# A two-layer retention/attention/MoE step: modulation by chunks in the first stage, a split scatter, and norms on two columns

## The chip, the core and the metric

The kernel runs on one core of a Trainium2 chip. A core has five engines with a queue each: PE (TensorE, the matrix engine; its weight loads are listed apart as PEld), DVE (VectorE), ACT (ScalarE), POOL (GpSimd) and SP (SyncE, which here only issues DMAs). They meet through semaphores. All memory traffic runs over 16 DMA engines that the queues share. The metric is the time of one execution on the device in microseconds (us), the median of the runs.

## What is computed

256 tokens (128 of a prompt, 128 of a sample) with 1024 channels go through two layers, everything in float32. Cut to what matters here:

```python
def trunk_layer(x, cond, lw, lam_init, ropes, ctx):
    mod = (jax.nn.silu(cond) @ lw['w_ada'] + lw['b_ada'])[:, None, :]
    shift1, scale1, gate1, shift2, scale2, gate2 = jnp.split(mod, 6, axis=-1)
    h = rmsnorm(x, lw['norm_mix']) * (1 + scale1) + shift1
    mix, new_ctx = token_mixers(h, lw, lam_init, ropes, ctx)   # retention | differential | latent attention
    x = x + gate1 * (mix @ lw['w_out'])
    h = rmsnorm(x, lw['norm_ffn']) * (1 + scale2) + shift2
    x = x + gate2 * moe_ffn(h, lw)                             # 64 experts, 6 per token, and a shared one
    return x, new_ctx
# at the end: y = rmsnorm(x, norm_final), for prompt and sample
```

`w_ada` is 1024 x 6144 in each layer, 24 MB; `w_in` is 1024 x 2208; an expert has three weights of 1 MB, and all 64 experts of both layers are read.

## The kernel before

The order of every engine's work is written out by hand: each engine has one function, and named semaphores tie them together.

**Tiles.** Activations lie transposed: `xT` and `hT` hold eight chunks of 128 channels, each 128 partitions x 256 tokens (prompt and sample beside each other). Weights of the mixer pass through a ring `gu` of four slots of 2 MB. `stream_items` lists the pieces in the order of loading: `("ada", l, q)`, one twelfth of `w_ada` of a layer; `("w_in", l, k)`, 512 columns of `w_in` (k = 2: queries and keys of the differential attention; 3: its values and the query latent; 4: 160 columns, the key latent; 0 and 1: retention); `("mla", l, 0)`, the two up-projections of latent attention; `w_out`; the shared expert. Item n goes into slot n % 4, and SP issues its load only when PE has counted (`weights_used`) the use of item n - 4. SP issues in order, so one waiting load holds back all behind it.

**First stage, layer 0.** DMAs: `xT`, then all constants `cst` (968 KB), then items. Items 0 to 3 are the four quarters of the first third of `w_ada`, by rows: a quarter has 256 of the 1024 input channels for all 2048 columns (shift 1 and scale 1). Only when all four are in PSUM is a modulation value complete. PE does `norm(0)` (the sums of squares by 8 matmuls with a matrix of ones), `ada(0..3)` and a select (L1483: matmuls that sum the four partial rows and turn them), DVE adds the bias and makes `amp`, and ACT (prompt half) and DVE (sample half) modulate the eight chunks of `hT` (L759, L1019). Then `w_in` 2 (queries and keys, 32 matmuls of 256 columns, L1528), `ada` 4 and 5, `w_in` 3 for the prompt (8 matmuls of 512 columns), the differential scores of unit 0 (L1566) with two rotations, `w_in` 3 for the sample (8 more), scores of unit 1 with the turning of the softmax of unit 0 (L1465) between their halves, `ada` 6 and 7, `w_in` 4, and so on.

**The softmax beside it.** Between the scores of unit 0 and those of unit 1 stand a chain on DVE (maximum, rope: `d_roped`) and one over ACT and DVE (`exps(0)`, then `combined(0)`: `p_scaled`). The scores of unit 1 wait for `d_roped`, the turning of unit 0 for `p_scaled`.

**Norms.** `norm(k)`: k = 0 and 2 at the start of a layer, k = 1 and 3 ahead of its experts. For odd k the squares are summed on DVE to one chunk, one matmul with ones spreads the sums over all partitions (L1509), ACT takes the root of 128x256 (L749), DVE the reciprocal (L1011), and the chunks are scaled (L1015) and modulated. PE fills the time with four matmuls of 512 columns (L1518).

**Experts.** Per layer 22 rounds: two with fixed experts, then ten turns of a "quad" (four experts, 32 token slots each) and a "pair" (two experts, 64 slots each). `expert_round` does gate and up (L1954), a gather for the next round (L1886), the scatter of the round before (L1893, 8 matmuls), turns, and down (L1983). SP loads the experts in an order that the routing gave, each part when its buffer is free.

**End.** After the last scatter DVE adds into `xT` (L1440, 16 instructions), PE turns `xT` back (first all chunks of the prompt, then the sample), ACT squares four halves (L964), takes the root (L967), DVE scales with the final gain into a strided layout (L1453, twice 128x1024), and ACT issues two stores (L971).

Of the kernel before, what the change touches and what calls it, by code (L numbers as in the profile page):

```python
# [29 lines left out]
P = 128  # L30
# [44 lines left out]
CONSTS = ["ident", "ones", "rot_d", "rot_m", "cos_d", "sin_d", "cos_m", "sin_m", "fwd", "bwd", "before", "iota", "cols",  # L75
          "order"]
CO = {n: P * i for i, n in enumerate(CONSTS)}
COL = {"i+1": 0, "C-i": 1, "C-1-i": 2, "i": 3, "eps": 4, "sel": 5, "first": 13, "cap": 16}


FIRST_W = len(CONSTS) * P + G * NC_ + DEPTH * 6 * NC_ + 4 * NC_
# [3 lines left out]
def shape_constants():  # L85

    a = np.zeros((P, len(CONSTS), P), np.float32)
    i = np.arange(P)
    a[:, 0] = np.eye(P)
    a[:, 1] = 1.0  # L90
# [19 lines left out]
    a[:, 2], a[:, 4], a[:, 5] = tables(P // DIF_D, 0, DIF_D)  # L110
    a[:, 3], a[:, 6], a[:, 7] = tables(1, MLA_N, MLA_R)
    a[:, 8] = np.maximum(i[None, :] - i[:, None], 0)
    a[:, 9] = np.maximum(i[:, None] - i[None, :], 0)
    a[:, 10] = i[:, None] < i[None, :]
    a[:, 11] = i[None, :] + 1
    a[:, 12, 0], a[:, 12, 1], a[:, 12, 2], a[:, 12, 3], a[:, 12, 4] = i + 1, P - i, P - 1 - i, i, EPS
    for j in range(4):
        for g in range(G):
            a[32 * j + g, 12, 5 + G * j + g] = 1.0

    first = np.maximum(FIXED - i, 0) * 1e6 + (P - i)
    a[:, 12, 13] = first
    cap = np.full(E, PAIR_CAP)
    rank = np.arange(E)
    for m in range(TURNS):
# [3 lines left out]
    a[:, 12, 16:16 + E] = cap  # L129
    a[:, 13, 0:E], a[:, 13, E:2 * E] = first[:E], rank  # L130
    return a.reshape(P, len(CONSTS) * P)
# [5 lines left out]
ADA_AT = [{"P2": [4, 5], "P3": [6, 7], "P4": [8], "UQ": [9], "M": [10, 11], "P0a": [12], "P0b": [13],  # L137
           "P1a": [14], "P1b": [15]},
# [3 lines left out]
THIRD = 2048  # L142


def stream_items():
# [5 lines left out]
    for l in range(DEPTH):  # L151
        if l == 0:
            out += [("ada", n // 12, n % 12) for n in range(4)]
        if 2 * l in ADA_NORM:
            out.append(("ada", 1, ADA_NORM[2 * l] % 12))
        for k in (2, 3, 4):
            out.append(("w_in", l, k))
            ada(l, f"P{k}")
# [14 lines left out]
def trunk(nc, t, out):  # L173
    ctx = ExitStack()
    with ctx:
# [15 lines left out]
        at = CO["order"] + P  # L191
# [107 lines left out]

        key_row, above, chosen = (hit[0:E, E * n:E * n + E] for n in range(3))  # L300
# [47 lines left out]
        def bc(ap, axis, n):  # L348
# [13 lines left out]
            ada_r ada_sel ada_mod  # L362
            sq_ready sq_summed ss_ready std_ready xn_ready h_a h_d amp_ready
# [11 lines left out]
            turned_y y_sq y_ms y_std y_done act_own dve_own""".split()  # L375
# [14 lines left out]
        for l in range(DEPTH):  # L390
            off = 0 if l == 0 else expert_slot[l - 1][1]
            for n in range(starts[l], ends[l]):
                item_slot[n] = (off + n - starts[l]) % RING
# [1721 lines left out]
```

## Time and profile before

| | |
|---|---|
| median of 3 runs | 1363.7 us (1361.63 to 1365.36) |
| the profiled execution's own time | 1363.03 us |
| its span | 1361.0 us |
| PE busy | 1238.2 us (91%) |
| DVE, ACT busy | 283.1 us (21%), 233.1 us (17%) |
| DMA | 496.14 MB, mean 365 GB/s |

The span runs from the first to the last recorded instruction; 2.0 us of the execution lie outside it. The chain of waits goes back from the last instruction to the first, and only what stands in it can shorten the run. In 40 slices of the span the DMA engines read 411 to 422 GB/s while the experts run, and less in the two mixers (154 to 287 GB/s in the slices from 0.08 to 0.17 of the span, 152 to 257 in those from 0.50 to 0.62); the first mixer runs to about 197 us.

### The profile page before, as it was taken

Reading aid. Unit: us, or ns where it says so; the run is one execution under the profiler, and the core shown is the slowest. Engines: PE = TensorE matmul, PEld = TensorE weight load, DVE = VectorE, ACT = ScalarE, POOL = GpSimd, SP = SyncE. Lnnn points to the kernel's source line nnn. Section 1 sums busy time; section 2 is a strip of 40 time slices with the busy share of each in tenths; the row PEclk is TensorE's granted clock in tenths of the full one; section 3 lists DMA queues with packets and bytes.
Section 4 is the critical chain, followed back from the end, with each engine's and each line's share of the span. In section 5 each row is a group of like instructions: output and inputs, shape, how many; then the busy total and the mean of one; then the engine's idle time right before and its main releaser. Section 6 shows DMA issues by size and latency. Waiting matters only on the chain.

```text
span 1361.0 us, 22696 instructions
## 1 busy us (share of the span) xinstructions
PE 1238.2 (91%) x9592; PEld 843.2 (62%) x9592; DVE 283.1 (21%) x714; ACT 233.1 (17%) x516; POOL 2.7 (0%) x13
## 2 busy tenths in 40 slices
PE   4999999999998898889899999999999889888986
PEld 2656578667765565556565658766767565555654
DVE  1253344111010110011033624511011010101012
ACT  1243312110100010000034521311010001000101
POOL 0000000000000000000000000000000000000000
PEclk9999999999998898889999999999999899999988
DMA  9886739899999999999965653999999999999991
GB/s 389 359 346 255 287 154 411 360 421 421 420 421 421 422 421 422 422 422 421 409 231 221 257 213 152 417 372 414 421 420 421 422 421 422 422 422 421 422 414 72
DMA packets 81024, 496.14 MB, mean 365 GB/s; under 512 B 10560, under 2 KB 12864, under 8 KB 24640
## 3 DMA queue, kind: packets, MB, share of 16 engines
q1 hardware_dynamic: 76752, 492.68, 88.3%
q10 hardware_dynamic: 4208, 2.52, 0.6%
q8 instruction: 51, 0.84, 0.2%
q14 instruction: 13, 0.11, 0.0%
HBM read 493.17 MB, written 2.00 MB: 364 GB/s over the span
## 4 chain that ended last, share of the span: by engine, by line
PE 66%; DMA 29%; SPq 2%; DVE 1%; issue 1%; ACT 0%; DVEq 0%
DMA dn<-in_exp_w_down 18%; PE PS L1954 14%; PE PS L1983 12%; PE PS L1528 8%; PE PS L1886 7%; PE PS L1893 6%; DMA gu<-in_exp_w_gate 6%; PE PS L1790 4%; DMA gu<-in_w_in 2%; PE PS L1496 2%; PE PS L1465 2%; PE PS L1852 2%; DMA gu<-in_w_ada 2%; PE PS L1930 1%; SPq L504 1%
## 5 line engine op out<-in xcount | busy, mean ns | idle before, releaser
L1954 PE MATMUL PS<-gu,arena 128*32 128x256 f32 (+1 forms) x3072 | 314.6, 381 | 1.8 <-issue 1.8
L1983 PE MATMUL PS<-arena 128*64 128x512 f32 (+1 forms) x336 | 177.9, 679 | 62.2 <-DMA dn<-in_exp_w_down 60.7
L1954 PEld LDWEIGHTS PS<-gu,arena 128*32 128x32 f32 (+1 forms) x3072 | 185.4, 117 | 78.3 <-issue 19.9
L1983 PE MATMUL PS<-dn,arena 128*32 128x512 f32 (+1 forms) x688 | 185.7, 637 | 0.0
L1886 PE MATMUL PS<-arena 128*128 128x128 f32 x1408 | 176.3, 278 | 0.5 <-ACT arena L936 0.5
L1886 PEld LDWEIGHTS PS<-arena 128*128 128x128 f32 x1408 | 164.1, 192 | 17.9 <-issue 16.7
L1893 PE MATMUL PS<-arena 128*128 128x256 f32 x704 | 159.6, 380 | 1.4 <-ACT arena L918 1.4
L1954 PE MATMUL PS<-arena 128*64 128x256 f32 (+1 forms) x672 | 151.9, 379 | 0.0
L1893 PEld LDWEIGHTS PS<-arena 128*128 128x128 f32 x704 | 130.4, 190 | 19.8 <-ACT arena L918 3.2
L1383 DVE TENSOR_TENSOR arena<-arena,PS 128x256 f32<-128x256 f32 x44 | 18.5, 421 | 558.3 <-ACT arena L932 558.3
L918 ACT ACTIVATE arena<-PS 128x512 f32<-128x512 f32 x88 | 52.6, 597 | 463.5 <-PE PS L1983 463.5
L1983 PEld LDWEIGHTS PS<-arena 128*64 128x64 f32 (+1 forms) x336 | 44.2, 143 | 116.5 <-issue 113.7
L1954 PE MATMUL PS<-xh,arena 128*64 128x256 f32 x352 | 82.1, 387 | 19.3 <-DMA gu<-in_exp_w_gate 19.2
L1954 PEld LDWEIGHTS PS<-arena 128*64 128x64 f32 (+1 forms) x672 | 83.4, 124 | 20.3
L1954 PEld LDWEIGHTS PS<-xh,arena 128*64 128x64 f32 x352 | 47.3, 139 | 55.8 <-DMA gu<-in_exp_w_gate 22.9
L1983 PEld LDWEIGHTS PS<-dn,arena 128*32 128x32 f32 (+1 forms) x688 | 48.3, 127 | 45.6 <-issue 42.8
L1377 DVE COPY arena<-PS 128x512 f32<-128x512 f32 x44 | 30.4, 691 | 214.5 <-PE PS L1465 214.5
L932 ACT ACTIVATE arena<-PS 128x256 f32<-128x256 f32 x44 | 16.9, 384 | 314.3 <-PE PS L1954 314.3
L1528 PE MATMUL PS<-gu,xh 128*128 128x512 f32 (+1 forms) x192 | 66.0, 498 | 0.5 <-DMA gu<-in_w_in 0.5
L1528 PE MATMUL PS<-xh,gu 128*128 128x256 f32 x256 | 60.2, 397 | 3.1 <-DMA gu<-in_w_in 1.9
L1528 PEld LDWEIGHTS PS<-xh,gu 128*128 128x128 f32 x256 | 50.5, 199 | 13.1 <-DMA gu<-in_w_in 4.1
L1496 PE MATMUL PS<-gu,condw 128*32 128x512 f32 x384 | 46.9, 614 | 6.7 <-DMA gu<-in_w_ada 6.1
(241 smaller groups left out, 964.8 us busy)
## 6 DMA issues: line engine op xcount, KB each, us to landing
gu<-in_exp_w_gate SPq DMA_DIRECT2D x106, 1024.0 KB, 16.0
gu<-in_exp_w_up SPq DMA_DIRECT2D x86, 1024.0 KB, 17.6
dn<-in_exp_w_down SPq DMA_DIRECT2D x86, 1024.0 KB, 18.5
gu<-in_w_ada SPq DMA_DIRECT2D x24, 2048.0 KB, 10.7
arena<-in_exp_w_up SPq DMA_DIRECT2D x42, 1024.0 KB, 14.5
arena<-in_exp_w_down SPq DMA_DIRECT2D x42, 1024.0 KB, 16.1
xh<-in_exp_w_gate SPq DMA_DIRECT2D x22, 1024.0 KB, 11.3
gu<-in_w_in SPq DMA_DIRECT2D x8, 2048.0 KB, 12.0
```

The lines of the kernel that those rows point to most:

```text
L918: return A(yy[:, :, half], PS[:, 7 - n, :].rearrange("p (t c) -> p c t", c=NC_), ACT.Copy)
L1377: return v.tensor_copy(turned_back, PS[:, 6, :])
L1383: tt(hh, sact, PS[:, 5, FF:2 * FF], ALU.mult).then_inc(S["hid_ready"], 1)
L1465: return pe.transpose(dst, src, ident[0:parts, 0:parts])
L1496: ins = mmul(PS[32 * j:32 * j + 32, 7, :], condw[:, 2 * quarter + c, :], wv[:, c, 512 * j:512 * j + 512], start=(quarter == 0 and c == 0), ...
L1528: ins = mmul(PS[0:lhs(k).shape[-1], bank, o:o + rhs(k).shape[-1]], lhs(k), rhs(k), start=(k == 0), stop=(k == NC_ - 1))
L1790: ins = mmul(PS[:, wo_bank(c), (c % 2) * T:(c % 2) * T + T], wo[k // 4][:, k % 4, c], mixT[:, k] if k < 4 else latent_T[:, k - 4], start=( ...
L1852: ins = mmul(PS[:, bank, j * T:j * T + T], w[:, u, k, j], hT[:, k, :], start=(k == 0), stop=(k == NC_ - 1))
L1886: ins = mmul(PS[:, 4, (c % 4) * P:(c % 4) * P + P], h_tok[:, g, c], onehot[b][:, g], start=(g == 0), stop=(g == 1))
L1893: ins = mmul(PS[:, c // 2, (c % 2) * T:(c % 2) * T + T], yy[:, c], selT, start=(first and c % 2 == 0), stop=False, skip_group_check=True)
L1954: ins = mmul(PS[w * h:w * h + w, 5, FF * half:FF * half + FF], xg[:, k, w * h:w * h + w], weights[half][:, k], start=(k == 0), stop=(k == ...
L1983: ins = mmul(PS[w * h:w * h + w, 7 - n, :], hidT[:, j * P + w * h:j * P + w * h + w], weights[:, j, 512 * n:512 * n + 512], start=(j == 0) ...
```

## The change

It has four parts.

1. **First stage of layer 0.** The first third of `w_ada` is laid out by columns (`w_ada_first`): a piece has all 1024 input channels for two chunks of 128 channels of shift and scale. PE makes two chunks' modulation from one piece (`chunks(i)`, L1717) and selects it with four matmuls of 2 columns (`chunks_select(i)`, L1725); DVE and ACT then modulate these two chunks. `w_in` 2 and 3 are loaded behind the first two pieces, and PE takes both projections chunk by chunk as `hT` comes (L1738, L1749). The second value product, which stood behind the scores of unit 0, now stands ahead of them. The constants are split: 264 KB first, the other 704 KB (`tables_in`) with the late ones. The `ada` pieces have new places: before, 4 and 5 stood behind `w_in` 2, 6 and 7 behind the scores of unit 1, 8 behind `w_in` 4 and 9 ahead of the last queries; now 4 and 5 behind the scores of unit 1, 6 and 7 behind `w_in` 4, 8 and 9 ahead of the last queries, 12 moves behind the second half of `w_in` 0 and 14 to the end.
2. **Norms 1 and 3.** The sums come as two columns (128x2), root and reciprocal are taken of these, and two matmuls spread them into PSUM; DVE reads the factors there. The four filling matmuls become five, in three places.
3. **Last turn of a layer's experts.** The scatter is split: five of its 8 matmuls between gate and up of the last pair, three behind up. SP issues the last pair's gate and up of its second expert ahead of the down weights of its first.
4. **End.** PE turns `xT` back in the order of the additions. The root's table is loaded ahead of the squares. For the prompt DVE multiplies PSUM by the gain before the root is known, and ACT scales; for the sample one DVE instruction as before. Both read PSUM with a stride of 128 elements and write SBUF in order. ACT and SP store one half each.

```diff
-ADA_AT = [{"P2": [4, 5], "P3": [6, 7], "P4": [8], "UQ": [9], "M": [10, 11], "P0a": [12], "P0b": [13],
-           "P1a": [14], "P1b": [15]},
+ADA_AT = [{"P3": [4, 5], "P4": [6, 7], "UQ": [8, 9], "M": [10, 11], "P0b": [12, 13], "P1b": [14, 15]},
...
+FIRST_USED = [("chunks", 0, 0), ("chunks", 0, 1), ("chunks", 0, 2), ("chunks", 0, 3), ("w_in", 0, 2), ("w_in", 0, 3)]
...
+            out += [("chunks", 0, 0), ("chunks", 0, 1), ("w_in", 0, 2), ("w_in", 0, 3), ("chunks", 0, 2), ("chunks", 0, 3)]
+            ada(l, "P3")
...
                     if n - starts[l] >= RING:
-                        sp.wait_ge(S["weights_used"], n - RING + 1)
+                        sp.wait_ge(S["weights_used"], freed_by[it])
...
+                    queries_and_keys((0, 1, 2, 3))
+                    values_and_latent((0, 1))
+                    chunks(2)
+                    values_and_latent((2,))
+                    chunks_select(2)
+                    values_and_latent((3,))
+                    chunks(3)
+                    queries_and_keys((4, 5))
+                    chunks_select(3)
+                    values_and_latent((4, 5))
+                    queries_and_keys((6, 7), told=True)
+                    values_and_latent((6, 7), told=True)
...
+                for g in range(G):
+                    ins = mmul(PS[:, 5, 2 * g:2 * g + 2], hT[:, 0, g * P:g * P + P], C("ones", 2), start=True, stop=True)
                 ins.then_inc(S["ss_ready"], 1)
+                fill(1)
+                pe.wait_ge(S["rstd_ready"], k // 2 + 1)
+                for g in range(G):
+                    ins = mmul(PS[:, 5, T + g * P:T + g * P + P], small[:, G + g:G + g + 1].to_broadcast([P, P]), ident,
+                               start=True, stop=True)
...
+                        if last and half == 0:
+                            pe.wait_ge(S["y_out"], m * 4 + 2 * (r0 + u))
+                            scatter(cs=range(5))
...
                 for part in range(3):
                     sp.wait_ge(used[part], r0 + ROUNDS - 1)
                     load_pair(0, l, xl, part)
+                    if part == 1:
+                        load_pair(RING, l, xf, 2)
...
-            for g in range(G):
-                stt(y_tok[:, g].rearrange("p (t c) -> p c t", c=NC_),
-                    PS[:, 4 + 2 * g:6 + 2 * g, :].rearrange("p b (c t) -> p (b c) t", c=4), small[:, 6 + g:7 + g],
-                    final_gain.rearrange("p (t c) -> p c t", c=NC_), ALU.mult, ALU.mult).then_inc(S["y_done"], 1)
+            tt(y_gained.rearrange("p (t c) -> p t c", c=NC_), by_token(0), gain, ALU.mult).then_inc(S["y_gained"], 1)
+            v.wait_ge(S["sq_ready"], 2 * DEPTH * NC_ + 4)
...
+            stt(y_tok[:, 1].rearrange("p (t c) -> p t c", c=NC_), by_token(1), small[:, 7:8], gain, ALU.mult,
+                ALU.mult).then_inc(S["y_sample"], 1)
```

What PE has in its queue around the scores of unit 0 (the 128x128 products of `arena`), before; the rows of 128x512 are the value products, those with `condw` are `ada` pieces:

```order
L1528 MATMUL PS<-gu,xh 128x512 x7
L1566 MATMUL PS<-arena 128x128 [waits dk_ready]
L1566 MATMUL PS<-arena 128x128 x3
L1634 MATMUL PS<-arena,cst 128x256
L1635 MATMUL PS<-arena,cst 128x256
L1566 MATMUL PS<-arena 128x128 [waits s_half]
L1566 MATMUL PS<-arena 128x128 x3
L1528 MATMUL PS<-gu,xh 128x512 x8
L1566 MATMUL PS<-arena 128x256 [waits caches_placed,d_roped]
L1566 MATMUL PS<-arena 128x256
L1465 MATMUL PS<-cst,xh 128x128 [waits p_scaled]
```

And the same place now:

```order
L1749 MATMUL PS<-gu,xh 128x512 [waits h_d,h_a] x3
L1650 MATMUL PS<-arena 128x128 [waits dk_ready,dq_ready]
L1650 MATMUL PS<-arena 128x128 x3
L1787 MATMUL PS<-arena,cst 128x256 [waits cq_raw,tables_in]
L1788 MATMUL PS<-arena,cst 128x256
L1650 MATMUL PS<-arena 128x128 [waits s_half]
L1650 MATMUL PS<-arena 128x128 x3
L1650 MATMUL PS<-arena 128x256 [waits caches_placed,d_roped,cq_raw]
L1650 MATMUL PS<-arena 128x256
L1542 MATMUL PS<-cst,xh 128x128 [waits p_scaled]
```

The eight value matmuls between the second half of the scores and the wait for `d_roped` are gone from there; they stand ahead of the scores.

SP's queue in the first mixer before, from the first load to the two of `mla` (in brackets the count of ring pieces that must have been used):

```order
L590 DMA gu<-in_w_ada 128x2x2048 x4
L595 DMA gu<-in_w_in 128x8x512 [waits weights_used]
L580 DMA late<-in_packed_late 128x3344
L590 DMA gu<-in_w_ada 128x2x2048 [waits weights_used] x2
L595 DMA gu<-in_w_in 128x8x512 [waits weights_used]
L590 DMA gu<-in_w_ada 128x2x2048 [waits weights_used] x2
L595 DMA gu<-in_w_in 128x8x160 [waits weights_used]
L590 DMA gu<-in_w_ada 128x2x2048 [waits weights_used] x2
L606 DMA gu<-in_mla_w_uq 128x2x768 [waits weights_used]
L608 DMA gu<-in_mla_w_ukv 128x1024
```

And now:

```order
L615 DMA gu<-in_w_ada_first 128x4096 x2
L624 DMA gu<-in_w_in 128x8x512 x2
L615 DMA gu<-in_w_ada_first 128x4096 [waits weights_used] x2
L604 DMA cst<-in_packed_first 128x1408
L606 DMA late<-in_packed_late 128x3344
L619 DMA gu<-in_w_ada 128x2x2048 [waits weights_used] x2
L624 DMA gu<-in_w_in 128x8x160 [waits weights_used]
L619 DMA gu<-in_w_ada 128x2x2048 [waits weights_used] x4
L635 DMA gu<-in_mla_w_uq 128x2x768 [waits weights_used]
L637 DMA gu<-in_mla_w_ukv 128x1024
```

Both `w_in` pieces have moved ahead of the third and fourth modulation piece, and between the 160 columns of `w_in` 4 and `mla` there are four `ada` pieces where there were two. Those four are `ada` 6 to 9; the second of them (7) goes into the slot that `ada` 4 leaves.

## Rows read from the trace of the kernel before

**Rows 1.** The page: shares of the chain that ended last, by engine.

```profile
PE 66%; DMA 29%; SPq 2%; DVE 1%; issue 1%; ACT 0%; DVEq 0%
```

**Rows 2.** Chain of waits, its last part, in order of time: start us, us, what.

```profile
1352.11 1.28 ACT L967
...
1353.41 0.30 ACT small L967
...
1353.73 0.18 DVE small L1449
```

**Rows 3.** Timeline, first mixer: start us, us, engine, line, op, tiles, count [idle before <-releaser].

```profile
32.03 1.06 PE L1483 MATMUL PS<-cst,rada 128*128 128x8 f32 x8 [0.70 <-ACT rada L734]
34.28 15.74 PE L1528 MATMUL PS<-xh,gu 128*128 128x256 f32 x64 [1.19 <-DVE xh L1019]
61.16 0.72 PE L1566 MATMUL PS<-arena 32*128 32x128 f32 x8
63.52 7.13 PE L1528 MATMUL PS<-gu,xh 128*128 128x512 f32 x16
68.88 1.14 DVE L1085 SCALAR_TENSOR_TENSOR xh<-xh,small 128x128 f32<-128x128 f32 x4
72.43 3.64 PE L1496 MATMUL PS<-gu,condw 128*32 128x512 f32 x32
87.60 1.97 PE L1681 MATMUL PS<-arena,gu 128*96 128x256 f32 x8 [0.53 <-DMA gu<-in_mla_w_ukv]
116.57 8.86 PE L1528 MATMUL PS<-xh,gu 128*128 128x256 f32 x32 [1.95 <-DMA gu<-in_w_in]
```

**Rows 4.** DMAs by line: count, issue ns, issued when; under each its time to landing.

```profile
L590 SPq DMA_DIRECT2D gu<-in_w_ada x2: 473/501/529, 2.9 to 3.4; - x2
DMA to landing us min/median/max: 20.1/22.3/24.5
...
L590 SPq DMA_DIRECT2D gu<-in_w_ada x1: 374/374/374, 70.7 to 70.7; - x1
DMA to landing us min/median/max: 7.5/7.5/7.5
...
L608 SPq DMA_DIRECT2D gu<-in_mla_w_ukv x1: 469/469/469, 76.5 to 76.5; - x1
DMA to landing us min/median/max: 11.0/11.0/11.0
```

**Rows 5.** Windows: us, busy of PE, PEld, DVE, ACT, POOL, PEclk, DMA share, GB/s.

```profile
34.25:38.00 3.75, 3.72 (x11) 3.03 (x12) 1.98 (x8) 2.63 (x7) 0.61 (x2) 0.62 0.97 409
255.00:260.00 5.00, 5.00 (x45) 1.94 (x48) 0.69 (x1) 1.19 (x2) 0.00 (x0) 1.00 0.47 164
1302.70:1309.10 6.40, 6.35 (x20) 1.96 (x21) 0.00 (x0) 0.60 (x1) 0.00 (x0) 0.56 1.02 424
```

**Rows 6.** Timeline around the norm ahead of layer 0's experts.

```profile
199.33 0.70 PE L1509 MATMUL PS<-xh,cst 128*128 128x256 f32 x2 [1.90 <-DVE xh L1265]
200.57 1.75 DVE L1011 RECIPROCAL small<-small 128x256 f32<-128x256 f32 x1 [1.30 <-ACT small L749]
203.52 4.63 PE L1840 MATMUL PS<-w_rt,xh 128*128 128x64 f32 x32
```

**Rows 7.** Timeline, start of the last pair of layer 0 and of layer 1.

```profile
674.08 0.40 PE L1954 MATMUL PS<-xh,arena 128*64 128x256 f32 x1 [1.08 <-DMA gu<-in_exp_w_gate]
...
1327.57 0.40 PE L1954 MATMUL PS<-xh,arena 128*64 128x256 f32 x1 [0.15 <-DMA gu<-in_exp_w_gate]
```

**Rows 8.** Timeline at the end.

```profile
1353.94 3.99 DVE L1453 SCALAR_TENSOR_TENSOR arena<-PS,small,arena 128x1024 f32<-128x1024 f32 x2
...
1357.96 0.34 ACTq L971 DMA_DIRECT2D out_y_sample<-arena  x1
```

**Rows 9.** Lines: strided PSUM reads on ACT, and 128x1024 in order on DVE.

```profile
L918 ACT ACTIVATE arena<-PS x88: 597/597/598, 238.8 to 1343.3; 128x512 f32<-128x512 f32 x88
...
L1062 DVE TENSOR_TENSOR xh<-xh,small x6: 1224/1226/1227, 114.1 to 800.2; 128x1024 f32<-128x1024 f32 x6
```

More of the change, by code:

```diff
@@ L681, in _ @@
                     load_quad(0, l, xs[0], 2)
-                    for part in range(3):
+                    for part in range(2 if last else 3):
                         load_pair(RING, l, xf, part)
+                    return xf
+                with sp.Fori(0, TURNS - 2) as m:
+                    turn_loads(m, lambda x: bass.ds(m * PER_TURN + x, 1))
+                m = TURNS - 2
+                xf = turn_loads(m, lambda x: slice(m * PER_TURN + x, m * PER_TURN + x + 1), last=True)
                 xl = expert_in(sp, l, slice(pair_at(TURNS - 1) + 1, pair_at(TURNS - 1) + 2))
@@ L748, in norm @@
                 act.wait_ge(S["ss_ready"], k + 1)
-                A(small[:, 0:T], PS[:, 5, 0:T], ACT.Sqrt, bias=col("eps"), scale=1.0 / D).then_inc(S["std_ready"], 1)
-                if k == 0:
-                    for n in range(4):
-                        ada(n)
+                sums = (small[:, 0:G], PS[:, 5, 0:2 * G:2]) if k % 2 else (small[:, 0:T], PS[:, 5, 0:T])
+                A(*sums, ACT.Sqrt, bias=col("eps"), scale=1.0 / D).then_inc(S["std_ready"], 1)
                 if k in ADA_NORM:
@@ L1489, in ada @@
                 third, quarter = divmod(n, 4)
-                if quarter == 0 and third > 0:
-                    pe.wait_ge(S["ada_r"], third)
+                if quarter == 0:
+                    if third == 1:
+                        pe.wait_ge(S["chunk_r"], NC_ // 2)
+                    else:
+                        pe.wait_ge(S["ada_r"], third - 1)
                 wv = w.rearrange("p (c n) -> p c n", c=2)
@@ L1888, in gather, with scatter @@
                     return ins
-                def scatter(told=None, first=False):
-                    for c in range(NC_):
+                def scatter(told=None, first=False, cs=range(NC_)):
+                    for c in cs:
                         ins = mmul(PS[:, c // 2, (c % 2) * T:(c % 2) * T + T], yy[:, c], selT,
@@ L1960, in expert_round @@
                         gather(1 - b, 0).then_inc(S["gathered"], 1)
[L1962 removed]
+                    if last:
+                        scatter(cs=range(5, NC_))
+                    elif u > 0:
                         pe.wait_ge(S["y_out"], m * 4 + 2 * (r0 + u))
```

321 lines of the change are left out of this document (211 added, 110 removed).

## The prediction, on record before the kernel ran

> **What bounds the kernel now.** I read the chain of waits by engine first: PE holds two thirds of it and DMA nearly all the rest [rows 1], so DVE and ACT count only where PE waits for them. Then I read the chain in order of time: in the first mixer DMA and PE alternate in it, in the experts mostly DMA and PE, and only its last ten microseconds lie on ACT and DVE (a table load, a root, a reciprocal [rows 2]). Then the timeline, for what PE waits for: 0.53 us for `mla`, 1.95 us for `w_in` 0 [rows 3], both DMAs that were issued late because their ring slot was still in use. Then the times to landing [rows 4], which give the pitch of the pieces: two that were issued together landed after 20.1 and 24.5 us, 0.5 us apart in issue, so 4.9 us per piece of 2 MB. Then windows, for the granted clock: 0.62 in the stretch that follows PE's wait for the modulation, 0.56 in the one after the wait for an expert's down weights [rows 5]. In the expert stage DMA sets the pace, but its queue still has holes early in the stage (share 0.47 at 255 to 260 us [rows 5]) that end when PE frees buffers. So whatever moves the end of the first mixer moves the rest of the run by as much.
>
> **First stage.** The four parts do not touch each other, so they add up. This one is the large one, and I follow PE through it.
>
> Start of the projections. Before, the fourth `ada` piece landed at 3.4 + 24.5 = 27.9, and the first product ran at 34.28 [rows 3, 4], 6.4 us behind. Now only two pieces come ahead of `w_in`, and 704 KB of constants fewer: 27.9 - 2 x 4.9 - 1.7 + 5.9 = 22.3 (the 1.7 is 704 KB at the same pitch, the 5.9 the 6.4 less a margin, since the modulation is no longer behind the DMA). A gain of 12.
>
> To the scores of unit 0. The same 64 + 32 instructions now run in one piece: 15.74 for queries and keys (its slow clock at the start kept, as PE is idle just before 22.3 too), two times 7.13 for the values, 2 x 1.8 for the two chunk pieces between (3.64 for two [rows 3]), and 1 to 1.8 for two selects (1.06 each at most [rows 3]). Sum 35.1, so 57.4 against 61.16 before. A gain of 3.8 only, but with 7.1 us of values done and two `ada` pieces (3.6) not yet done: 7.3 in work.
>
> The lost cover. Before, scores of unit 0 to scores of unit 1 held the second value product, 7.13 us [rows 3], and the two chains of the softmax ended under it: the last operation of `combined(0)` ended at 68.88 + 1.14 = 70.02, 6.4 after the scores ended at about 63.6. Those chains have not become shorter. The scores now end at 57.4 + 2.4 = 59.8; the turning waits for 66.2, and with it and the second half of the scores (1.3) PE comes to `ada` 4 at 67.5. Before it was at 72.43. The gain in work is 4.9 - 3.6 = 1.3. So PE idles about 5.8 us of 6.4, in two parts, and I expect the granted clock to fall after it as it did at 34 us; half of a slow stretch falls on `ada` 4, which then takes 2.6 instead of 1.8. It leaves its slot at 70.1.
>
> The ring. This is the step that decides. In that slot goes `ada` 7, and SP is in order, so `ada` 8 and 9 and `mla` come behind it. By then the queue is empty: the last load ahead, `ada` 6, was issued at 57 to 60 and needs 7.5 us. A load into an empty queue lands after 7.5 (issued 70.7); from the issue at 70.7 to the landing of `mla` (76.5 + 11.0 = 87.5) were 16.8 us, with two `ada` pieces in them [rows 4]. Now there are three: 16.8 + 4.9 = 21.7, so `mla` lands at 91.8. PE is there long before: from 76.07 to 87.07 were 11.0 us with one `ada` and its select; now two `ada`s without (+0.8), after `ada` 4 and 5: 67.5 + 4.4 + 11.8 = 83.7. A wait of 8 us against 0.53.
>
> After the wait. Before, 87.60 to the end of the `ada` pieces at 114.6 took 27.0, with a wait of 0.9 that now goes (its softmax ends under the DMA). Now one more `ada` and a select (+2.8), and a slow clock for some 5 us after the long wait (+2.4): 31.3, so `w_in` 0 starts at 123.1. It landed long ago (its slot is that of `ada` 9, not of `mla`), so the wait of 1.95 is gone, and its first half takes 7.1 instead of 8.86 [rows 3]: done at 130.2 against 125.4. From there PE has no idle stretch before and the same instructions after. **+4.8 us.**
>
> Its bounds. If the clock never falls: -0.8 and -2.4. If pieces behind an empty queue land 0.5 earlier: -0.5. Low end +1. If the slow clock lasts twice as long after the wait and `w_out` 0, which now waits for `w_in` 1's slot, comes a little late: high end +7.5.
>
> **Norms 1 and 3.** From the one matmul at 199.33 to the router at 203.52 are 4.2 us: 0.7 matmul, some 0.5 root, 1.75 reciprocal [rows 6], the rest handovers and scaling. Root and reciprocal of 2 columns take 0.30 and 0.18 in the last norm [rows 2]; against it stand two matmuls and a handover, 0.7 to 0.9, and the narrow matmul is 0.3 shorter. 0.3 + 0.17 + 1.57 - 0.85 = 1.2 us each. The five fillers could delay the router: two end ahead of the sums (PE idles 1.90 there), one lies under the root, two end at about 202.7, and the router, paced by the chunks, ends when the last chunk does. It passes to the end, as the DMA holes after it (2.6 us at 255 to 260 alone [rows 5]) take it up. 2 x 1.2: **-2.4**, bounds -3.2 and -1.2.
>
> **Last turn.** The pair waited 1.08 us for its gate in layer 0 and 0.15 in layer 1 [rows 7]. With 1 MB of down weights taken from ahead of it, it lands 2.5 us earlier, and PE's own order is next. The split scatter moves 8 matmuls, adds none, and PE was busy in that whole stretch; it would only cover a late up. **-1.1**, bounds -1.3 and 0.
>
> **End.** The table load leaves the path: -1.28 [rows 2]. One of three squares leaves it: -0.6. But DVE has the prompt's product in front of the sum: it starts when the third square is done and takes 1.23 (128x1024 in order [rows 9]), so the sum starts about 0.7 later than the squares alone would let it. Then one DVE instruction of 1.25 stands where two of 2.04 stood (3.99 [rows 8]): -2.8. The stores now run at once, the second half MB behind the first, a quarter of a piece's pitch: +1.2. Sum with handovers -1.28 - 0.6 + 0.7 - 2.8 + 1.2 = **-2.7**. The last store was issued at 1357.96, 3.0 before the span's end [rows 8]; now at about 1354.3. What is not shown is DVE reading PSUM with a stride of 512 bytes. The nearest row is ACT reading PSUM with a stride of 32 bytes, 597 ns for 512 columns, as a plain copy [rows 9]; L1453 itself has strides in SBUF and takes 2.04. I take 1.25; at 2.04 both instructions are 0.8 longer and this part is -1.1. Bounds -3.3 and -1.0.
>
> The Trainium skill ("SBUF — State Buffer", Door 1: The DMA port swizzle, the note on cachelines) says that SBUF is free of penalty only within 16 bytes and that PSUM has lines of 8 bytes, and that PSUM patterns which are not contiguous slow matmuls significantly. The first explains the 2.04 of L1453; the second speaks against this part of the change, which moves the stride into PSUM. By it the part would be worth -1.1, and ACT's 597 ns speaks against it.
>
> **Sum.** +4.8 - 2.4 - 1.1 - 2.7 = -1.4 on an execution of 1363.03, so 1361.6; that execution lies 0.7 below the median, so 1362.0.
>
> **Rivals.**
> - *The ring does not bind* (`mla` is there, or the slot is free early). For it: the first stage gains 7.3 us of work by 57 us, and DMA is idle from 65 us. Against: the issue order above. Then the wait of 8 and its slow clock go, a part returns further on: the stage is worth -3 to -5, total about 1353. Chance 0.15.
> - *The clock does not fall*, all else as forecast: +1 to +1.8 for the stage, total 1358.5. Against: rows 5, where it fell after waits of 2 to 5 us. 0.17.
> - *The slow clock lasts*: after 8 us without work PE stays at the lower level through all products of `mla`, which keeps each later slot in use longer, and `w_out` 0 comes late too. +9 or more for the stage, and the end gives 1.1 only: 1368 and above. It decides from about 5 us of further slow work, where rows 5 show 2 to 3. 0.10.
> - *The PSUM stride costs*, the rest as forecast: 1363.6. 0.13.
> - Forecast 0.45.
>
> **Range and chances.** What a measurement of this kernel can tell from no change is about 0.3%, 4.1 us: 1359.6 to 1367.8. The forecast's own range is 1358 to 1366. With the first two rivals in part, 1355 to 1367. Faster: the first two rivals (0.15 + 0.13) and a small part of the forecast, 0.34; slower 0.12; same 0.54.
>
> **What would show it.** A gap on PE of some 6 us just ahead of the second unit's scores, with a DVE instruction as releaser; `mla` landing near 92 with a PE gap of about 8 before it, and DMA idle near 65 to 72; `w_in` 0 without a wait, near 123; end of the first mixer near 202. Router start 1.2 earlier behind the sums. No gap at the last pair. No table load behind the squares, DVE instructions of 1.2. Wrong if the `mla` gap is under 3 us, or if the first mixer ends before 197.

## The result, and the profile after

The changed kernel took 1368.03 us in the median of 13 runs against 1363.43 of the kernel before beside it: ratio 1.0034, interval 1.0024 to 1.0044. I had forecast 1362.0 and a range up to 1367. The profiled execution took 1366.16, the lowest of the 13, with a span of 1364.3; before, it was 1363.03 with 1361.0. So the two traces hold 3.3 us of the 4.6.

The chain by engine, from the page of the changed kernel: the share of DMA fell [rows 1]. The chain before held 15.43 and 14.49 us of the gate loads of the two last pairs and 56.2 us of loads of `w_ada` and `w_in` in the first mixer; now it holds none of the former and 18.8 of the latter. PE's own work has taken their place in it, so the share says nothing of where the time went.

```profile
PE 70%; DMA 25%; DVE 2%; SPq 2%; issue 1%; ACT 1%; DVEq 0%; ACTq 0%
```

Timeline of the first mixer after (start us, us, engine, line, op, tiles, count, idle before and its releaser), the places of [rows 3]:

```profile
21.62 8.86 PE L1738 MATMUL PS<-xh,gu 128*128 128x256 f32 x32 [0.27 <-DMA gu<-in_w_in]
...
56.95 0.72 PE L1650 MATMUL PS<-arena 32*128 32x128 f32 x8
...
63.07 0.43 DVE L1208 TENSOR_TENSOR arena<-arena 128x256 f32<-128x256 f32 x1
...
63.60 1.23 PE L1650 MATMUL PS<-arena 32*128 32x256 f32 x4 [4.22 <-issue]
...
65.88 1.11 PE L1542 MATMUL PS<-cst,xh 128*128 128x128 f32 x4 [1.05 <-DVE xh L1155]
...
68.07 4.57 PE L1574 MATMUL PS<-gu,condw 128*32 128x512 f32 x32
...
92.68 3.73 PE L1837 MATMUL PS<-arena,gu 128*96 128x256 f32 x8 [8.21 <-DMA gu<-in_mla_w_ukv]
...
100.42 0.66 PE L1542 MATMUL PS<-cst,xh 128*128 128x128 f32 x4 [0.93 <-DVE xh L1155]
...
124.73 7.17 PE L1618 MATMUL PS<-xh,gu 128*128 128x256 f32 x32
```

PE starts early, idles beside the softmax of unit 0, comes to `ada` 4 when DMA has nothing left to bring, and waits 8.21 us for `mla`. The profile puts the gap of 4.22 us down to "issue", but it ends 0.1 us behind the last operation of `d_roped` (L1208, done at 63.50), for which PE waits in its program: this one is the wait for the softmax's chain. PEclk, the third last column of the windows (us, busy of PE, PEld, DVE, ACT, POOL, PEclk, DMA share, GB/s) shows the granted clock at its lower level, 1.2 GHz (0.50 of full speed), behind both gaps, and the second and third row show DMA with nothing to do:

```profile
66.00:68.00 2.00, 2.00 (x8) 1.09 (x8) 0.00 (x0) 0.60 (x1) 0.00 (x0) 0.50 0.03 8
68.00:70.00 2.00, 2.00 (x14) 0.59 (x16) 1.40 (x2) 0.28 (x1) 0.00 (x0) 0.50 0.00 0
70.00:72.00 2.00, 2.00 (x22) 0.48 (x16) 0.20 (x2) 1.98 (x9) 0.00 (x0) 1.00 0.00 0
...
90.00:92.00 2.00, 0.00 (x0) 0.00 (x0) 0.00 (x0) 0.00 (x0) 0.00 (x0) 0.50 1.06 432
...
94.00:96.00 2.00, 2.00 (x6) 1.36 (x5) 0.00 (x0) 0.00 (x0) 0.00 (x0) 0.50 0.79 328
```

Norm 1 and the router after, the places of [rows 6]:

```profile
205.98 0.61 PE L1601 MATMUL PS<-cst,xh 128*128 128x2 f32 x4 [0.18 <-DVE xh L1335]
...
206.92 0.17 DVE L1069 RECIPROCAL small<-small 128x2 f32<-128x2 f32 x1 [0.99 <-ACT small L793]
...
209.56 4.24 PE L1996 MATMUL PS<-w_rt,xh 128*128 128x64 f32 x32
```

The last pair in layer 1 after, where [rows 7] had a wait for DMA, and its down product:

```profile
1331.67 0.43 PE L2110 MATMUL PS<-xh,arena 128*64 128x256 f32 x1
...
1333.02 0.38 PE L2110 MATMUL PS<-xh,arena 128*64 128x256 f32 x1
1334.40 0.38 PE L2110 MATMUL PS<-xh,arena 128*64 128x256 f32 x1 [1.01 <-issue]
...
1345.46 0.64 PE L2144 MATMUL PS<-arena 128*64 128x512 f32 x1 [0.79 <-DVE arena L1447]
```

The wait is gone, but PE now stands still in the midst of the gate, and the releaser is "issue": no semaphore explains it. The end after, against [rows 2, 8]:

```profile
1356.94 1.23 DVE L1525 TENSOR_TENSOR xh<-PS,arena 128x1024 f32<-128x1024 f32 x1 [1.35 <-ACT xh L1019]
...
1358.80 1.28 DVE L1531 SCALAR_TENSOR_TENSOR arena<-PS,small,arena 128x1024 f32<-128x1024 f32 x1
...
1360.11 0.36 SPq L729 DMA_DIRECT2D out_y_sample<-arena  x1
```

Read at the same instructions, the two traces give how far the changed kernel lies behind:

| place | before | after | behind |
|---|---|---|---|
| first projection | 34.28 | 21.62 | -12.7 |
| `ada` 4 | 72.43 | 68.07 | -4.4 |
| first product with `mla` | 87.60 | 92.68 | +5.1 |
| first half of `w_in` 0 done | 125.43 | 131.90 | +6.5 |
| sums of norm 1 | 199.33 | 205.98 | +6.65 |
| router's end, layer 0 | 208.15 | 213.80 | +5.65 |
| last pair's gate, layer 0 | 674.08 | 679.58 | +5.5 |
| last pair's down, layer 0 | 686.08 | 692.57 | +6.5 |
| projections' end, layer 1 | 724.28 | 730.15 | +5.9 |
| router's end, layer 1 | 860.71 | 865.57 | +4.9 |
| last pair's gate, layer 1 | 1327.57 | 1331.67 | +4.1 |
| last pair's down, layer 1 | 1339.59 | 1345.46 | +5.9 |
| end of the span | 1361.0 | 1364.3 | +3.3 |

Two places lose: the first mixer, and from gate to down of each last pair (12.0 us in both layers before, 13.0 and 13.8 after).

One row of the kernel before may not be typical of it. Its first half of `w_in` 0 took 8.86 us [rows 3], at a clock of 0.57 up to 120 us. Two kernels that run the same first stage, e4 and e10 below, took 7.17 behind as long a wait:

```profile
116.70 7.17 PE L1573 MATMUL PS<-xh,gu 128*128 128x256 f32 x32 [2.02 <-DMA gu<-in_w_in]
```

```profile
116.44 7.17 PE L1528 MATMUL PS<-xh,gu 128*128 128x256 f32 x32 [2.14 <-DMA gu<-in_w_in]
```

They reached the sums of norm 1 at 197.77 and 197.52. Against them the changed kernel is 8.2 to 8.5 us behind there, not 6.65.

All ratios below are against the kernel before, with the interval.

### The profile page after: what moved, and what is told of

Same layout as the page of the kernel before. It is cut to its first block, busy times and chain, and to the rows that moved or that the text cites. A ratio compares the mean times of both kernels' runs of the same rounds, so it can differ in the third digit from the quotient of the medians.

```text
span 1364.3 us, 22780 instructions
## 1 busy us (share of the span) xinstructions
PE 1243.4 (91%) x9624; PEld 845.4 (62%) x9624; DVE 279.4 (20%) x720; ACT 236.2 (17%) x521; POOL 2.6 (0%) x13
## 4 chain that ended last, share of the span: by engine, by line
PE 70%; DMA 25%; DVE 2%; SPq 2%; issue 1%; ACT 1%; DVEq 0%; ACTq 0%
DMA dn<-in_exp_w_down 18%; PE PS L2110 15%; PE PS L2144 12%; PE PS L2042 8%; PE PS L1618 7%; PE PS L2049 7%; PE PS L1946 4%; DMA gu<-in_exp_w_gate 4%; PE PS L1574 2%; PE PS L1542 2%; PE PS L2008 2%; DMA gu<-in_w_in 1%; PE PS L1738 1%; PE PS L1749 1%; PE PS L2086 1%
## 5 line engine op out<-in xcount | busy, mean ns | idle before, releaser
L1618 PE MATMUL PS<-gu,xh 128*128 128x512 f32 (+1 forms) x160 | 51.7, 478 | 0.0
L1618 PE MATMUL PS<-xh,gu 128*128 128x256 f32 x192 | 43.6, 383 | 1.8 <-DVE xh L1081 1.8
L1618 PEld LDWEIGHTS PS<-xh,gu 128*128 128x128 f32 x192 | 35.6, 190 | 10.5 <-issue 5.8
L1618 PEld LDWEIGHTS PS<-gu,xh 128*128 128x128 f32 x160 | 26.7, 190 | 22.3 <-issue 21.8
## 6 DMA issues: line engine op xcount, KB each, us to landing
dn<-in_exp_w_down SPq DMA_DIRECT2D x86, 1024.0 KB, 18.8
```

Source lines behind the costliest of these rows:

```text
L1618: ins = mmul(PS[0:lhs(k).shape[-1], bank, o:o + rhs(k).shape[-1]], lhs(k), rhs(k), start=(k == 0), stop=(k == NC_ - 1))
```

## Experiments

**The first mixer.** e1 puts the cover back: `values_and_latent` takes one block of tokens at a time, and block 1 (g=1) comes behind the scores of unit 0.

```
-    def values_and_latent(ks, told=False):
+    def values_and_latent(ks, told=False, g=0):
 ...
-    pe.wait_ge(S["cq_raw"], 2)
+    values_and_latent(range(NC_), told=True, g=1)
```

> The changed kernel, with one thing of the first stage put back: the second block of 128 tokens gets its values and latent behind the scores of unit 0 (in bank 5), not ahead of them. Theory A (the lost cover starts the loss: PE idles 4.2 + 1.1 us beside the softmax, its clock falls to half from 63 to 70 us, ada 4 leaves its slot late at 70.9, and ada 7 to 9 and mla, issued behind it, come late by as much): the 7 us of values lie beside the softmax again, no slow clock, ada 4 used at about 66, mla lands near 88 instead of 92.7, PE still waits some 7 to 8 us for it since it is early too; the first mixer ends 4 to 5 us earlier than in the changed kernel, so near 200, and the time is about 1.000 of the kernel before. Rival (the order of the pieces alone sets when mla lands, or the projections then wait for chunks 2 and 3 instead): the gain is under 2 us, ratio 1.002 to 1.0035.

Measured 1.0015 (1.0004 to 1.0026). `ada` 4 starts at 64.89 and takes 3.64 for both pieces, without a slow clock; the sums of norm 1 are 2.2 earlier than in the changed kernel. That is under the 4 to 5 of theory A: with less work at hand PE waits 2.57 us for chunk 2, and `mla` gains 2.8 only.

```profile
33.28 3.22 PE L1714 MATMUL PS<-gu,condw 128*32 128x512 f32 x16 [2.57 <-DMA gu<-in_w_ada_first]
...
89.92 2.45 PE L1832 MATMUL PS<-arena,gu 128*96 128x256 f32 x5 [9.04 <-DMA gu<-in_mla_w_ukv]
```

The wait for `mla` is longer, not shorter: the cover is worth 2 us, the queue is the larger part. The ratio lies between theory A and the rival, as does the gain. The trace of e1 is of its slowest execution, 2.6 us above its median, so its end can't be set against the changed kernel's. e2, which moved `ada` pieces in PE's order as well, deadlocks and has no time. e5 changes the order of the loads and the slots that they go to, and nothing on PE.

```
+at8 = items.index(("ada", 0, 8))
+turned_slots = [0, 2, 3, 1]
...
-item_slot[items[n]] = n % RING if n < len(FIRST_USED) else (off + n - starts[l]) % RING
+raw = raw_of(l, off, n)
+item_slot[items[n]] = turned_slots[raw] if n >= at8 else raw
...
+items[at8:at8 + 3] = [("mla", 0, 0), ("ada", 0, 8), ("ada", 0, 9)]
```

> The changed kernel with another order of loads alone: mla is loaded ahead of ada 8 and 9 instead of behind them, in the slot that ada 5 leaves; PE's order is the same. Theory A (the ring and the order of the pieces set when mla lands): ada 7 is issued at 71, mla at about 73 when ada 5 is used, and lands 7.5 + 4.4 after 71, near 83; PE comes to it at 84.5 and does not wait, the 8.2 us and the slow clock from 92 to 97 us go, ada 8 and 9 land near 88 and 93 before PE needs them at about 92 and 95; the first mixer ends 8 to 10 us earlier than in the changed kernel, near 195, so the run is at about 0.997 of the kernel before. Rival (all bytes up to w_in 0 have to come anyway, and PE's wait only moves to ada 8, 9 or w_in 0): waits of 6 us or more there, ratio 1.002 to 1.0035.

Measured 0.9955 (0.9943 to 0.9967), and the same places as above (L1847 is the first product with `mla`, and the profile shows no gap before it):

```profile
85.29 0.70 PE L1660 MATMUL PS<-arena 32*128 32x256 f32 x4
85.92 1.97 PE L1847 MATMUL PS<-arena,gu 128*96 128x256 f32 x8
...
91.41 0.66 PE L1552 MATMUL PS<-cst,xh 128*128 128x128 f32 x4 [0.93 <-DVE xh L1165]
```

No wait for `mla`, no slow clock (1.97 and not 3.73 for eight products), and no wait later: the last projection ends at 194.88, and the sums of norm 1 start at 196.78, 9.2 earlier. The bytes are the same, so the order of three loads, with their slots, was worth the whole loss of the stage and more (0.7 to 1.0 us more even against e10 and e4). The ratio is better than the 0.997 of theory A.

**The last pair.** e3 undoes the split of the scatter.

```
-    if last and half == 0:
-        pe.wait_ge(S["y_out"], m * 4 + 2 * (r0 + u))
-        scatter(cs=range(5))
...
-    if last:
-        scatter(cs=range(5, NC_))
-    elif u > 0:
+    if u > 0:
```

> The changed kernel with the whole scatter behind the up product of the last pair again, as before; loads and all else stay. In the trace of the changed kernel the last pair takes 13.0 us (layer 0) and 13.8 us (layer 1) from its first gate product to its down product, against 12.0 in both layers before. Theory A (the split itself costs: products of other banks and weights between gate and up): 12.0 us in both layers, and the run is some 2 to 2.8 us shorter than the changed kernel, ratio 1.0015. Rival B (PE runs out of instructions: a block of them is fetched at 1331.5 us, when the gate products have begun, and PE stands still from 1333.4 to 1334.4; before, the block came at 1326.5, ahead of the gate): where the block ends has nothing to do with the split, so a stop of 0.4 to 1.2 us stays in or near the gate, the pair takes 12.4 to 13.2 us, and only 0.3 to 0.6 us of the two layers come back, ratio 1.003.

Measured 1.0028 (1.0016 to 1.0040); from gate to down 12.9 and 13.7 us, and the stops stay:

```profile
1335.42 0.38 PE L2110 MATMUL PS<-xh,arena 128*64 128x256 f32 x1 [1.28 <-issue]
```

Rival B had it. The stops were 0.27 us longer than in the changed kernel; with the stops taken off, the last pair took 12.78 us in both layers with the split and 12.43 without. So the split costs 0.35 in each layer, as it does in e4, which has no stop (12.35 in both layers against 12.0). The rest goes with the stop. So the place of the code was tried. e6 adds 16 small matmuls near the start of PE's program.

```
+    for _ in range(16):
+        mmul(PS[:, 7, 0:32], ident, cst[:, 0:32], start=True, stop=True)
```

> The changed kernel with 16 small matmuls (128x32) more on PE, ahead of the first chunk, where PE waits for the DMA anyway; all that comes behind them in PE's program stands 16 matmuls later. Theory B (PE runs out of instructions in the gate of the last pair, since its program skips the branch for overflow and comes out some 12 matmuls before the end of a block of instructions): 16 further on it comes out at the start of the next block, the stop in the gate goes, and the last pair takes 12.35 us from gate to down in both layers, as in the run without the first stage, against 13.0 and 13.8; 1.5 to 2.2 us less than the changed kernel, ratio 1.002. Rival (not the place in the program but the loads that run at that time delay the block): 13.0 and 13.8 stay, ratio 1.0034.

Measured 1.0100 (1.0086 to 1.0115). Neither: the stops grew to 3.24 and 3.82 us and moved ahead of the gate, which then ran with a slow clock (5.3 us instead of 3.6). That the place counts fits this run, since nothing but these 16 matmuls was added, where PE waits anyway; my reading of where a packet ends was wrong. e7, beside it, adds two fillers in norm 2.

```
     ins.then_inc(S["ss_ready"], 1)
+    if k > 0:
+        fill(2)
```

> As e6, and two filler matmuls (128x512, 1.7 us at full clock) behind the sums of norm 2, where the change took out four and PE now waits 1.8 us for DVE. Theory (the 1.8 us without work cost a slow clock in the projections behind it, which took 21.9 us instead of 20.9): the start of the projections stays, they take 20.9 again, 0.9 us less than e6. Rival (the projections were longer by chance, for another reason such as late weights): no difference from e6, or 0.2 more where the fillers end late.

Measured 1.0093 (1.0078 to 1.0107), not to be told from e6: the projections took 21.88 us in both, and PEclk was 1.00 in all of their windows in both. They are longer than before; DVE was busy without a break in the first 4 us of them in e7 and PE did 17 matmuls there, against 20 in each of the next two stretches of 4 us, so I put it down to PE being paced by DVE's chunks, which was not tried by itself. The theory of a slow clock there fell.

e9 and e10 shift the code by the same edit, in the changed kernel and in the kernel before. No work and no order changes, but the fourth turn is written out.

```
-    for m in range(DOWN_TURN + 1):
+    for m in range(DOWN_TURN + 2):
...
-    with pe.Fori(DOWN_TURN + 1, TURNS - 1) as m:
+    with pe.Fori(DOWN_TURN + 2, TURNS - 1) as m:
```

> The changed kernel with the fourth turn of the experts (m = 3) written out in PE's program instead of run in its loop: the same work in the same order, only what comes behind stands 176 matmuls later. So far the stop at the last pair followed one number, how many matmuls PE's program has ahead of the end of the overflow branch: 1642 and 1646 none, 1658 a stop of 1.7 us in the gate, 1662 of 0.2 to 0.9, 1674 and 1678 of 2.9 to 3.2 us right ahead of it, and the profile shows PE's program coming in packets of 16 KB. If 64 matmuls fill a packet, 1838 stands where 1646 + 3 x 64 = 1838 does, among the good places, and the second layer's as well. Theory B (place in the program): no stop, 12.35 us from gate to down in both layers, 2.1 us less than the changed kernel, ratio 1.0018. Rival (it hangs on the loads or the clock at that time, which e6 changed too): stops of 0.2 to 2 us stay, ratio 1.003 or more.

Measured 1.0042 (1.0024 to 1.0059): stops of 0.62 and 3.42 us ahead of the gates. They moved and grew again, so the count of 64 matmuls to a packet was wrong.

> The kernel before, with the fourth turn of the experts (m = 3) written out in PE's program instead of run in its loop: nothing else is changed, the work and its order are the same. Theory B (place in the program): PE comes out of the overflow branch in the second layer where e6 and e8 did, at the very start of a packet, and stands still for 3 to 4 us ahead of the gate, with a slow clock of 1.8 us behind it; in the first layer it comes out some 10 matmuls further on, between places with a full stop and places with none: 0 to 5 us. Sum 4 to 10 us slower than before, ratio 1.003 to 1.0075. Rival (the first stage's loads or PE's order cause the stops): none here, ratio 1.000.

Measured 1.0051 (1.0033 to 1.0069), for a kernel that has nothing of the change:

```profile
676.05 0.66 PE L1954 MATMUL PS<-xh,arena 128*64 128x256 f32 x1 [4.53 <-issue]
...
1334.13 0.66 PE L1954 MATMUL PS<-xh,arena 128*64 128x256 f32 x1 [3.78 <-issue]
```

This settles it against the rival: stops arise from where the code stands, without the first stage's loads or its order on PE. The row of the instruction queue (packets, MB, share) from 673 to 674 us in e10, within the stop from 671.5 to 676.05, and of the whole run of the changed kernel and of e10:

```profile
q8 instruction: 1, 0.02, 6.8%
```

```profile
q8 instruction: 51, 0.84, 0.2%
```

```profile
q8 instruction: 57, 0.93, 0.3%
```

The stop holds the arrival of one packet of 16 KB (0.84 MB over 51), and 352 matmul calls more (176 in each layer) are 6 packets more, so about 59 calls to a packet, an estimate (packets are counted whole, so 50 to 70 would fit). In the kernel before that packet came from 1326.8 on, 0.7 us ahead of the gate; in the changed one from 1332.0 on, when the gate had begun, 2.4 us before PE went on at 1334.40. That holds in all 22 stops of the table below: the first matmul behind the stop starts 2.3 to 2.9 us after the transfer of such a packet began (673.3 and 676.05 in layer 0 of e10, 680.3 and 682.60 in that of the changed kernel). A short stop is one in which PE still had matmuls to do for most of that time.

The stops of all runs, by what stands in PE's program ahead of the end of the overflow branch, counted in the built programs: matmul calls, and all of PE's instructions (layer 0, layer 1 in each column). The expectations give 4 to 16 calls fewer, and e1 four fewer than the changed kernel; those two have the same number.

| run | matmul calls | all instructions | stop, layer 0 | stop, layer 1 |
|---|---|---|---|---|
| before | 1650, 3292 | 1770, 3529 | none | none |
| e4 | 1654, 3296 | 1774, 3533 | none | none |
| changed; e3; e5 | 1666, 3308 | 1805, 3564 | 0.21; 0.48; 0.89 | 1.01; 1.28; 2.13 |
| e1 | 1666, 3308 | 1811, 3570 | 1.69 | 2.05 |
| e6 | 1682, 3324 | 1820, 3579 | 3.24 | 3.82 |
| e7 | 1682, 3326 | 1820, 3581 | 3.13 | 3.48 |
| e8 | 1682, 3326 | 1826, 3587 | 2.85 | 3.88 |
| e13 | 1710, 3352 | 1854, 3613 | 0.48 | none |
| e10 | 1826, 3644 | 1954, 3897 | 4.53 | 3.78 |
| e12 | 1842, 3660 | 1995, 3938 | none | 2.70 |
| e9; e11 | 1842, 3660 | 1989, 3932 | 0.62; 0.89 | 3.42; 3.35 |

**Put together.** e4 is the kernel before with all of the change but the first stage (no further edit).

> The kernel before, with all of the change but its first stage (norms, loads and split scatter of the last turn, end). By the two traces the first stage is worth +6.9 us at the end of the first mixer, and the rest -3.5. Theory A (the parts add up): the run is 3 to 4 us shorter than before, ratio 0.9975, span about 1357.5. Rival (the DMA queue of the experts gives back what is gained ahead of it: norm 1's 1.2 us were down to 0.2 at the last pair of layer 0): the gain of the norms does not reach the end and the late start hid some of it, so only -1 to -2, ratio 0.9990.

Measured 0.9960 (0.9946 to 0.9974), 1357.38 us in the median: more than theory A's 3.5, because the stops went with the first stage's code: 3.5 and the 2.1 that they cost make 5.6, and 0.40% is 5.5. So the first stage costs 8.2 us directly (205.98 against 197.77 at the sums of norm 1) and 2.1 by its place (12.99 and 13.79 in the last pairs against twice 12.35), 10.3 in all; the two ratios, 1.0034 and 0.9960, are 10 us apart. e8 took e1, e5, e6 and e7 together.

> The changed kernel with all four repairs: second block of values behind the scores of unit 0 (e1), mla loaded ahead of ada 8 and 9 (e5), 16 small matmuls as padding (e6), two fillers in norm 2 (e7). If they add up, e1's 2.5 us, e5's 8 to 10, e6's 2 and e7's 0.9: 14 us less than the changed kernel, 9 to 10 less than before, ratio 0.993. If e1 and e5 are two ways to the same gain (both bring mla earlier), e1 adds about 3 us of work done early, which w_in 0 or the later slots take back: then about 0.995.

Measured 0.9967 (0.9954 to 0.9980): sums of norm 1 at 193.95, 12.0 earlier than in the changed kernel, but stops of 2.85 and 3.88 us with slow gates took a good part of it. e11 is e5 with e3 and e9's edit, e12 is e11 with e1.

> The changed kernel with mla loaded ahead of ada 8 and 9 (e5), the scatter of the last pair in one piece (e3) and the fourth turn written out as in e9. By e5 the first mixer ends at 194.9, 9.4 us earlier than in the changed kernel; by theory B the last pairs take 12.0 instead of 13.0 and 13.8: another 2.8. Span 1364.3 - 12.2 = 1352, ratio 0.993. Rival: part of the start is taken back in the experts, where DMA sets the pace, as norm 1's gain was: 0.995 to 0.996, no better than e4 and e5.

Measured 0.9949 (0.9931 to 0.9967): the start is as forecast (sums of norm 1 at 197.37), the stops are 0.89 and 3.35 us, and the experts of layer 0 took 1.4 us more up to the last pair than in the changed kernel, stop aside, with one wait of 6.6 us for down weights where the other kernels have at most 5.5. e9, which has the late start, has the same wait, so it does not come of the early start. The rival came out right in size and, as far as these traces show, wrong in cause. This trace too is of the slowest execution, 3.8 us above the median.

> As e11, and the second block of values behind the scores of unit 0 (e1). Theory A: with the cover back ada 4 is used 3 us earlier, and since mla is now ahead in the queue all that follows moves too: first mixer end near 190 to 192, 2 to 4 us less than e11, ratio 0.990 to 0.9915. Rival: the ada pieces and w_in come no earlier, since DMA has no idle stretch left ahead of them, and PE waits for them instead (e8 waited 1.2 us for ada 7): within 1 us of e11.

Measured 0.9911 (0.9891 to 0.9932), 1353.04 us: sums of norm 1 at 191.98, 5.4 earlier than in e11, more than the 2 to 4 forecast. Theory A holds, with `ada` pieces waited for 1.10 and 0.93 us, as the rival had it in small.

```profile
75.33 1.92 PE L1581 MATMUL PS<-gu,condw 128*32 128x512 f32 x16 [1.10 <-DMA gu<-in_w_ada]
...
89.98 1.92 PE L1581 MATMUL PS<-gu,condw 128*32 128x512 f32 x16 [0.93 <-DMA gu<-in_w_ada]
```

The last run looked for a better place for e12's code; `padded` is true for the last quad of layer 0 alone.

```
+    for _ in range(44 if padded else 0):
+        mmul(PS[0:32, 5, 0:32], ident[0:32, 0:32], cst[0:32, 0:32], start=True, stop=True)
     pe.wait_ge(*downs_in)
```

> As e12 (values behind the scores of unit 0, mla ahead of ada 8 and 9, whole scatter), but the fourth turn is in PE's loop again, and 44 small matmuls (32x32) stand in layer 0 ahead of the last quad's down product, where PE waits 5 us for its weights. By e10 and e12, 352 matmul calls more are 6 packets of 16 KB more, so 58.7 calls a packet; the good places seen without written-out turns are 1642 to 1646 in the first layer and 3276 to 3280 in the second, e1 with 1658 and 3292 had stops of 1.7 and 2.0 us. 44 more give 1702 and 3336, one packet behind 1643 and 3277. Theory B: no stop in either layer, 12.0 us from gate to down in both, against e12's stop of 2.7 us in the second: 2 to 3 us less than e12, ratio 0.989. Rival (the packet's size or its start is not that, or the place hangs on more than this number): a stop of 1 us or more in one layer, no better than e12, 0.991 or more; if the small matmuls take more than the 5 us of the wait, up to 3 us more.

Measured 0.9922 (0.9900 to 0.9944), 1351.53 us, not to be told from e12 and short of the forecast 0.989. The stop of layer 1 went, 12.0 us from gate to down:

```profile
1317.84 0.43 PE L2115 MATMUL PS<-xh,arena 128*64 128x256 f32 x1
...
1329.85 0.64 PE L2146 MATMUL PS<-arena 128*64 128x512 f32 x1 [0.78 <-DVE arena L1454]
```

In layer 0 a stop of 0.48 stayed, and the 44 matmuls took 3.0 us of their own: the wait of 5 us is at the down product one round earlier (that of the pair ahead of the last quad), which I had misread.

## Why the prediction was wrong

*First stage, +4.8: measured +6.65.* The mechanism came out step by step: first projection 21.6 (22.3), scores 56.95 (57.4), turning 65.88 (66.2), `ada` 4 at 68.07 (67.5), `mla` product at 92.68 (91.8) after a wait of 8.21 (8). Two terms were short. `mla` landed 0.9 later than I had it. The step "with a wait of 0.9 that now goes (its softmax ends under the DMA)" failed: the 0.93 at 100.42 is there as before, and in e5 too, as the last part of that chain on DVE (L1164, at 97.84) waits for products that PE does behind the first ones of `mla`, and so behind the DMA. `w_in` 0 needed no wait, as said. So 1.9 of the error of the sum is here, within the bounds I had given. That holds against the one trace that I had read. The term "its first half takes 7.1 instead of 8.86" booked 1.7 us as a gain that e4 and e10 have without the change (7.17 in both); against them the stage is worth +8.2 to +8.5, beyond my high end of 7.5. e5 shows that the mechanism was the right one, and that the loss was not bound up with this stage.

*Norms, -2.4: measured -1.0 - 0.6 - 1.0 = -2.6.* Norm 1 gave 1.0 at the router's end (6.65 to 5.65), and the experts did not take it back (5.73 at the down product ahead of the last quad, 649.26 and 654.99). The -0.6 is norm 2, which the prediction left out: its four fillers went too, and the projections start 1.6 earlier and run 0.9 longer. That the sum came out at the forecast is luck in part: norms 1 and 3 gave 2.0 and not 2.4.

*Last turn, -1.1: measured +1.4.* This is the step that failed: "PE's own order is next". The waits of 1.08 and 0.15 us did go, and next came neither PE's order nor a load but PE's own instructions: stops of 0.21 and 1.01 us, with 0.4 more in each layer that e3 has too and that goes with a stop. And the split, priced at nothing ("moves 8 matmuls, adds none"), cost 0.35 in each layer; why was not tried. From the end of the last quad's down product to the pair's, layer 0 gained 0.15 and layer 1 lost 1.5. e10 shows the cause of the stops in a kernel without the change. Nothing in my sum could hold them: I priced what runs, and not where it stands.

*End, -2.7: measured -2.6.* The strided reads of PSUM took 1.23 and 1.28 us, as much as a read in order [rows 9], so the rival "the PSUM stride costs" is out. What went from the instruction is the stride in SBUF, and with it the time fell from 2.04 (one of the two in [rows 8]) to 1.28. The Trainium skill ("SBUF — State Buffer", Door 1: The DMA port swizzle) warns of patterns in PSUM that are not contiguous for matmuls; for a read by DVE no cost is seen here.

*The rest:* in layer 0 the down product ahead of the last quad, which runs with a slow clock behind its wait, took 0.9 longer (6.38 for 5.46), and the experts of layer 1 gave 0.5 back. 6.65 - 2.6 + 0.1 + 0.9 - 0.5 + 1.4 - 2.6 = 3.3. The other 1.3 of the median's 4.6 is not in these two traces. The stops differ between kernels with the same code on PE up to there (changed and e5: 0.21 and 0.89, 1.01 and 2.13), so they may differ between executions too, but that was not shown. A slip of the sum is smaller: 1361.6 and the 0.7 make 1362.3, not 1362.0, and in the chances the second rival is entered with 0.13 for its 0.17; neither changes the account above.

*Rivals.* "The slow clock lasts" named 1368 and had the right time for a wrong reason: the lower level lasted to about 97 us, 4 us of work, no longer than forecast. That 1368 came out was luck.

## What to carry to other kernels

Starting work early is of use only up to the next load that comes in order: look at which slot the next awaited piece needs and what is queued ahead of it, and move that piece first. Keep independent products for the place where a softmax or another chain leaves the engine alone. Where a program jumps over code that hardly ever runs, look for an "issue" gap right behind the jump, and when a small edit far away moves the time by some microseconds, compare that gap before anything else.

## What the runs showed of the hardware

PE's program comes in packets of 16 KB, by estimate some 59 matmul calls of this kernel, and behind a jump over the overflow branch PE stood still for 0.2 to 4.5 us and went on 2.3 to 2.9 us after the transfer of a packet had begun. In e10 it was the place of the code alone: 8.3 us of a run. The Trainium skill ("Runtime: NRT & Kernel Launch", Instruction fetch mechanics) states this mechanism: blocks of 16 KB, fetched ahead only in sequence, and a taken branch to code outside the two blocks at hand must wait for a fetch. The traces agree on the packet and on the jump; how much lies ahead of PE when it jumps they don't show. The same section says that full unrolling is preferred for this; e10 wrote out one turn more and got slower by 0.5%.

Open is the rule that tells a good place from a bad one. With the loop as in the kernel before, the stop grew with the number of calls ahead and was gone 44 calls behind e1's place in one layer; with a turn written out, places that should have been good by 59 calls a packet were bad. e10 has a turn of 176 calls more in each layer than the kernel before, by the estimate three packets, and has the longest stop. Other instructions than matmuls count too, and where a packet begins isn't shown. Open also is what the experts' loads add to a stop: DMA was busy for 83 to 89% of the stops of e6 and e10, and no run tried them with DMA idle.

Behind a stop of 4.53 us the granted clock was at 1.2 GHz for the next 5 us of full work, behind 2.70 us in e12 at 2.4 GHz throughout. A shorter stop doesn't mean a faster clock: behind the 2.13 us of e5 and the 2.05 of e1 in layer 1 the mean was 0.60 and 0.61 over the next 4.3 to 4.4 us, and behind the wait for `w_in` 0 of some 2 us it was 0.57 in the kernel before and 1.00 in e4. PE had been at work without a gap for at least 4 us before each of these.

```profile
1325.72 0.53 PE L2120 MATMUL PS<-xh,arena 128*64 128x256 f32 x1 [2.13 <-issue]
```
